# Row sums of the last two expert turns by slot-table products in both layers, and the first filters and spectrum inside the first expert loop

## The chip, the cores and the metric

The kernel runs on one core of a Trainium2 chip, in one launch. The metric is the device time of that launch in microseconds (us), as the median of several runs. All data is f32. The engines are TensorE (PE), VectorE (DVE), ScalarE (ACT), GpSimd (POOL) and SyncE (SP), each with its own instruction queue; they wait for each other by semaphores. DMAs are issued by SP, POOL and ACT.

## What is computed

One step of a trunk with two layers over 384 tokens (128 of a prompt, 256 of a sample) of width 1024. Layer 0 mixes tokens with a gated linear attention and an mLSTM, layer 1 with a Hyena long convolution, computed as a product of spectra. Behind each mixer stands a mixture of 16 experts, of which every token uses two.

```python
def _hyena_mixer(u, p, j):
    z = u @ p['hy_w_in'][j]
    ...
    v, x1, x2 = jnp.split(z.astype(f32), 3, axis=-1)
    kf = _hyena_filters(L, p, j)
    def long_conv(s, o):
        y = jnp.fft.irfft(jnp.fft.rfft(s, n=2 * L, axis=1) * kf[None, :, o], n=2 * L, axis=1)[:, :L]
        return y + bias[o] * s
    y = x2 * long_conv(x1 * long_conv(v, 0), 1)
    return y.astype(u.dtype) @ p['hy_w_out'][j]

def _hier_moe(u, p, l):
    ...
    hg = jnp.einsum('bld,edf->blef', u, p['moe_w_gate'][l])
    hu = jnp.einsum('bld,edf->blef', u, p['moe_w_up'][l])
    h = jax.nn.silu(hg) * hu * gates.astype(u.dtype)[..., None]
    return jnp.einsum('blef,efd->bld', h, p['moe_w_down'][l])

def _trunk(x, cvec, init_states, p):
    for l in range(DEPTH):
        h = _modulate(x, p['norm1_w'][l], sh1, sc1)
        mix = _rec_mixer(...) if l % 2 == 0 else _hyena_mixer(h, p, j)
        x = x + g1 * mix
        h = _modulate(x, p['norm2_w'][l], sh2, sc2)
        x = x + g2 * _hier_moe(h, p, l)
    return _rmsnorm(x, p['norm_f_w']), finals
```

Left out are a convolution with three taps between `z` and the split, and the choice of the experts (a group by argmax, the two best in it, and their weights as `gates`). The Hyena filters do not depend on the tokens: `h` is a small network of the positions, its last matrix is `hy_f_w3`, and the spectrum `kf` follows by products with tables of cosines and sines.

## The kernel before

An expert loop has 16 turns, one for each expert. The 13 experts behind the first three are taken in the order of how many tokens they have, so that a turn has a fixed number of slots for token rows: 96 (three tiles of 32), 64 or 32. Turn 13 has two tiles, turns 14 and 15 have one each; `PICKED` are turns 14 and 15. Token rows are written to `x_rows` in DRAM by slot, read back turn by turn, transposed by PE (`rows_t`), multiplied with gate and up weights (`gate_up`, in two halves of 32 records), then SiLU on ACT, product on DVE, a transpose (`hidden_t`) and `down`. The result of a turn lies in `ysb[:, p % 2]`, copied there by ACT (`rows_out`), with 32 slots in each quarter of the partitions: quarter q holds columns 256 q to 256 q + 255. SP stores it to `y_rows` in DRAM (`store`).

Weights go through a ring of six slots of 2 MB, three for even and three for odd turns, one piece of `down` weights in `uT`. SP issues all of their loads and the stores in one hand-written order: behind the products of turn p come the loads for turn p + 2, then `store(p)`. SP's DMAs run in one queue in this order.

At the end of the loop a token's two rows have to be added with their weights w1 and w2:

- In layer 0 (`token_rows`, `first_rows`, `combined`, `rows_back`, `add_rows`) turns 14 and 15 are stored like the others. POOL then gathers two rows for each token from `y_rows` with six indirect DMAs, ACT scales the first, DVE adds the second, PE transposes the sum, and DVE adds it to the residual stream `xT`. PE fills the time until the rows come with the first filters: `first_taps` and `filters` multiply the small network with `hy_f_w3` (ring slot 0, loaded behind the last expert), DVE scales by a decay into `hpm`, and `spectrum` makes ten products with the tables.
- In layer 1 turns 14 and 15 are not stored. `in_last` and `pick_table` on DVE find out during turns 1 to 3 which tokens have a row in these turns and make a table of slots, which PE transposes in turns 4 to 6 (`pick`). At the end the product of this table with `ysb` (`last_expert`) opens the sum of a token tile in four banks, each with a quarter of the columns, and products of the gathered rows with diagonals of w1 and w2 (`others`) close it. DVE multiplies by the gate, adds to `x_tok` and norms (`final_rows`).

After layer 0 follow the norm and the z products of Hyena (`wide(("z", m), ...)`, 24 times 8 matmuls), with `filters(1)` in front of them on PE. The PSUM banks are given out by `claim`, in an order written out by hand; an engine that wants to write a bank waits until its reader before is through. If more tokens fall on an expert than it has slots (`over > CAP`), a branch of its own computes the rest; it is not taken with the inputs at hand.

## Time and profile before

| | us |
|---|---|
| median of 3 runs | 1237.32 |
| lowest and highest | 1233.12 and 1238.73 |
| span of the profiled execution | 1246.0 |
| PE busy in it | 1118.7 |
| DVE, ACT, POOL busy | 370.7, 213.4, 140.7 |

The profile records one execution: for every instruction its engine, line, start and duration, and for idle time in front of it the engine or DMA whose semaphore ended it. A matmul in f32 leaves two records, a transpose one. The two expert loops run from about 356 to 627 and from 947 to 1218 us. PEclk is the clock granted to TensorE, as a share of its full 2.4 GHz.

### The profile page before, as it was taken

What the parts mean: (1) busy time and instruction counts of PE and PEld (TensorE: products, weight loads), DVE (VectorE), ACT (ScalarE), POOL (GpSimd) and SP (SyncE); (2) the same over time, 40 slices, a digit from 0 to 9 for tenths busy, and PEclk for the clock granted to TensorE, in tenths of its full rate; (3) what the DMA queues carried; (4) which work ended last, traced back from release to release, by engine and by line L of the source; (5) the groups of instructions that cost most, each with busy time, mean ns of one, the idle gap of its engine ahead of it and who ended that gap; (6) DMA issues with size and microseconds to landing.
All of it is one profiled execution on the core that took longest, in us unless ns stands there. A gap on an engine that the chain in (4) does not pass through costs nothing.

```text
span 1246.0 us, 23402 instructions
## 1 busy us (share of the span) xinstructions
PE 1118.7 (90%) x10195; PEld 626.8 (50%) x10195; DVE 370.7 (30%) x954; ACT 213.4 (17%) x449; POOL 140.7 (11%) x163
## 2 busy tenths in 40 slices
PE   5999999899989959898699999999998995989965
PEld 2443445555665525454336665545665553555534
DVE  3202332574341101101047222487624120110104
ACT  2003201320321101111024111121021110111102
POOL 1143100022120000000010000042232000000001
PEclk9899999899989979998879999999998997999988
DMA  9988755369559998999964211001485999899984
GB/s 382 391 294 297 298 201 207 138 210 408 204 199 364 387 379 340 386 399 402 399 224 166 75 61 68 1 0 68 163 356 214 367 383 394 329 389 399 405 360 152
DMA packets 73236, 338.22 MB, mean 271 GB/s; under 512 B 6834, under 2 KB 16593, under 8 KB 58348
## 3 DMA queue, kind: packets, MB, share of 16 engines
q1 hardware_dynamic: 61784, 299.93, 62.3%
q0 software_dynamic: 10864, 36.42, 8.4%
q8 instruction: 82, 1.34, 0.4%
q10 hardware_dynamic: 484, 0.35, 0.1%
q14 instruction: 22, 0.18, 0.0%
HBM read 313.97 MB, written 22.70 MB: 270 GB/s over the span
## 4 chain that ended last, share of the span: by engine, by line
PE 71%; DMA 16%; DVE 6%; ACT 2%; issue 2%; SPq 1%; another core or an unknown queue 1%; DVEq 0%; ACTq 0%
PE ps L2284 19%; PE ps L1995 18%; DMA ring<-in_moe_w_up 12%; PE ps L1917 11%; PE ps L2308 7%; PE ps L2510 3%; DMA ring<-in_ada_w 3%; PE ps L2217 2%; PE ps L1938 2%; DMA ring<-in_hy_f_w 2%; PE ps L2480 1%; PE ps L2321 1%; PE ps L2267 1%; PE ps L1910 1%; PE ps L2294 1%
## 5 line engine op out<-in xcount | busy, mean ns | idle before, releaser
L2284 PE MATMUL ps<-ring,work 128*32 128x256 f32 x4736 | 299.8, 393 | 73.4 <-DMA ring<-in_moe_w_up 65.5
L2284 PEld LDWEIGHTS ps<-ring,work 128*32 128x32 f32 x4736 | 149.6, 112 | 174.4 <-issue 88.8
L1995 PE MATMUL ps<-uT,ring 128*128 128x384 f32 x640 | 217.2, 496 | 2.4 <-DVE uT L1341 1.3
L1995 PEld LDWEIGHTS ps<-uT,ring 128*128 128x128 f32 x640 | 121.7, 194 | 88.0 <-issue 10.8
L2308 PE MATMUL ps<-ring,work 128*32 128x256 f32 x1728 | 102.9, 379 | 1.2 <-issue 1.2
L1763 DVE COPY work<-ps 128x128 f32<-128x128 f32 x74 | 21.5, 290 | 261.4 <-PE ps L2294 261.4
L1917 PE MATMUL ps<-ring,uT 128*128 128x512 f32 x192 | 84.3, 596 | 0.0
L1165 ACT ACTIVATE work<-ps 128x128 f32<-128x128 f32 x74 | 20.5, 278 | 359.3 <-PE ps L2284 346.8
L2308 PEld LDWEIGHTS ps<-ring,work 128*32 128x32 f32 x1728 | 56.1, 110 | 37.9 <-issue 1.5
L1759 DVE TENSOR_TENSOR work<-ps,work 128x128 f32<-128x128 f32 x74 | 21.6, 291 | 161.6 <-ACT work L1165 161.6
L901 POOL DMA_DIRECT2D work<-x_rows x30 | 15.4, 515 | 422.4 <-PE ps L2267 414.5
L1848 DVE SCALAR_TENSOR_TENSOR work<-ps,vecT,work 128x127 f32<-128x127 f32 x96 | 35.5, 412 | 92.4 <-ACT work L1248 91.6
L1917 PEld LDWEIGHTS ps<-ring,uT 128*128 128x128 f32 x192 | 36.1, 191 | 47.6 <-issue 47.6
L1938 PE MATMUL ps<-ring,silc 128*32 128x512 f32 x384 | 48.8, 640 | 5.5 <-DMA ring<-in_ada_w 4.3
L1171 ACT COPY work<-ps 128x256 f32<-128x256 f32 x74 | 27.5, 372 | 114.6 <-PE ps L2308 107.7
L2510 PE MATMUL ps<-uT,ring 128*128 128x384 f32 x128 | 43.3, 491 | 1.2 <-DVE uT L1895 1.2
L1910 PE MATMUL ps<-tab_common,work 128*128 128x128 f32 (+2 forms) x161 | 27.4, 306 | 16.1 <-DMA work<-in_t_pos 10.9
L1917 PE MATMUL ps<-work,ring 128*128 128x128 f32 (+3 forms) x256 | 39.7, 293 | 1.5 <-DVE ring L1882 0.8
L939 POOL TENSOR_TENSOR ring<-ring 128x1024 f32<-128x1024 f32 x4 | 13.6, 3403 | 216.4 <-DVE ring L1871 216.4
L1917 PEld LDWEIGHTS ps<-work,ring 128*128 128x128 f32 (+1 forms) x256 | 32.6, 190 | 8.9 <-PE ps L1917 2.5
L1910 PEld LDWEIGHTS ps<-tab_common,work 128*128 128x128 f32 (+2 forms) x161 | 22.5, 170 | 28.1 <-issue 17.1
L1917 PE MATMUL ps<-work 128*128 128x512 f32 x80 | 36.5, 608 | 0.0
(352 smaller groups left out, 1082.4 us busy)
## 6 DMA issues: line engine op xcount, KB each, us to landing
ring<-in_moe_w_gate SPq DMA_DIRECT2D x32, 2048.0 KB, 12.6
ring<-in_moe_w_up SPq DMA_DIRECT2D x32, 2048.0 KB, 17.6
ring<-in_ada_w SPq DMA_DIRECT2D x24, 2048.0 KB, 11.4
ring<-in_moe_w_down SPq DMA_DIRECT2D x22, 2048.0 KB, 23.3
uT<-in_moe_w_down SPq DMA_DIRECT2D x10, 1536.0 KB, 16.4
ring<-in_rec_w_in SPq DMA_DIRECT2D x6, 2048.0 KB, 23.8
ring<-in_hy_w_in SPq DMA_DIRECT2D x6, 2048.0 KB, 10.8
y_rows<-work SPq DMA_DIRECT2D x64, 96.0 KB, 10.9
```

The lines of the kernel that those rows point to most:

```text
L1171: free(act.copy(ysb[:, p % 2, i, :], bank((l, p, "Y", i))[:, 0:256]), (l, p, "Y", i))
L1759: free(v.tensor_tensor(hh[:, par, :], bank((l, p, "GU", i))[:, P:2 * P], sg[:, par, :], ALU.mult), (l, p, "GU", i))
L1763: free(v.tensor_copy(hT[:, (FIRST[p] + i) % 2, :], bank((l, p, "HT", i))[:, 0:P]), (l, p, "HT", i))
L1848: ins = v.scalar_tensor_tensor(dst[:, a0 + do:a0 + do + n], src[:, a0 + so:a0 + so + n], w, dst[:, a0 + do:a0 + do + n], ALU.mult, ALU.add)
L1910: ins = pe.transpose(bank(key)[0:n, at:at + p], src, ident[0:p, 0:p])
L1917: ins = pe.matmul(out, lhsT, rhs, start=(i == 0), stop=(i == n - 1))
L1938: ins = pe.matmul(bank(key)[32 * q:32 * q + 32, :], silc[:, 2 * two + k, :], w[:, k, q * 512:(q + 1) * 512], start=(two == 0 and k == 0), ...
L1995: ins = pe.matmul(bank(key)[0:rows, 0:T], w(k), uT[:, k, :], start=(k == 0), stop=(k == DC - 1))
L2217: done(pe.matmul(bank(key)[:], h2T[:, j * P:(j + 1) * P], w3[0:65, at:at + 512], start=True, stop=True), key)
L2284: ins = pe.matmul(bank(key)[32 * q:32 * q + 32, 0:2 * P].rearrange("p (a n) -> p a n", a=2), xg[:, u, k, 32 * i:32 * i + 32], ring[:, 3 * ...
L2308: ins = pe.matmul(bank(key)[32 * q:32 * q + 32, 0:256], hT[:, (FIRST[p] + i) % 2, 32 * k:32 * k + 32], w[:, q * 256:(q + 1) * 256], start= ...
L2510: ins = pe.matmul(bank(("ho", m))[:, 0:T], w[:, k, (m % 4) * P:(m % 4 + 1) * P], uT[:, k, :], start=(k == 0), stop=(k == DC - 1))
```

## The change

1. **Layer 0 now does as layer 1.** `in_last`, `pick_table` and the transposes of the table run in both layers. Turns 14 and 15 are stored in neither.
2. **Open row sums.** A bank ("sum", l, j, hf) holds 512 columns of a token tile j. In layer 0 `rows_back` opens it with plain matmuls by the identity (before: transposes), in layer 1 `others` does. `picked(0, j)` adds turn 14 and `picked(1, j)` turn 15. Between matmuls that use different quarters of the array's rows and write the same bank PE waits for its own last matmul (`settle`). `down` of turn 15 stands between the sums of tile 1 and tile 2.
3. **Store and gathers.** The store of turn 13 is issued by ACT (`store_last`) instead of SP. POOL's six gathers wait for it and no longer for turn 15; the loads into ring slots 0, 1 and 2 behind the loop get waits for the readers of what lies there meanwhile.
4. **First filters inside the loop.** The part of `hy_f_w3` for stage 0 is loaded by ACT in turn 6 into `w3s0`; `first_taps(0)` and `filter_weights(0)` run in turn 10. `filters(0)` stands in front of turn 14's `hidden_t` and `down`, and `spectrum(0)` between them and the products of turn 15. `first_taps(1..3)` stand in front of z, `filter_weights(1..3)` behind z 0 to 2, and `filters(1)` behind z 4.
5. **Overflow indices** go to a table of their own (`late`), so `in_last` has 17 chained steps instead of 9. The additions stand in front of the branch and what the branch computes is added once more. ACT's `preload_act_table` stands in front of the branch as well.

The core of the diff:

```diff
+        FILTERS_AT = 4
@@ SP, behind the loop
-                    store(p)
+                    if p < NE - 3:
+                        store(p)
...
-                if l == 0:
-                    for p in PICKED:
-                        store(p)
@@ POOL
-                    for u in range(2):
-                        pool.wait_ge(S(f"y{u}_stored"), 4 * 16 * (NE // 2 * (l + 1) - l))
+                pool.wait_ge(S("picks_known"), l + 1)
+                for u in range(2):
+                    pool.wait_ge(S(f"y{u}_stored"), 4 * 16 * STORED * (l + 1))
+                if l == 0:
+                    full(pool, (0, PICKED[0], "GU", 0))
...
+                        pool.indirect_dma_start(tok_rows[l][q][:, j, :], None, y_dram[0:BASES[PICKED[0]], :],
@@ ACT, behind turn 14's step of the loop
+                store_last()
+                rows_out(PICKED[0], 0)
+                if l == 0:
+                    full(act, (0, NE - 3, "Y", TILES[NE - 3] - 1))
+                    spectrum(0, K_ORDER[0])
+                    first_rows(0)
+                    first_rows(1)
+                silu(PICKED[1], 0)
+                if l == 0:
+                    first_rows(2)
+                act.preload_act_table(ACT.Sqrt)
...
+                rows_out(PICKED[1], 0)
+                if l == 1:
+                    final_squares(0)
@@ DVE, behind turn 14's step of the loop
+                if l == 0:
+                    filters(0)
...
+                hidden_t(PICKED[0], 0)
+                if l == 0:
+                    combined(0)
+                    combined(1)
+                hidden(PICKED[1], 0)
+                hidden_t(PICKED[1], 0)
...
+                if l == 0:
+                    combined(2)
+                    for j in range(NT):
+                        add_rows(j)
+                else:
+                    final_rows()
@@ PE
+                def rows_back(j):
+                    pe.wait_ge(S("y_sum"), j + 1)
+                    for hf in range(2):
+                        key = ("sum", 0, j, hf)
+                        opened(pe, key)
+                        for n in range(4):
+                            m = 4 * hf + n
+                            pe.matmul(bank(key)[:, n * P:(n + 1) * P], utok[:, j, m * P:(m + 1) * P], ident, start=(n == 0), stop=False)
+                def others(j):
+                    pe.wait_ge(S(f"token_rows_{j}"), 32 * (l + 1))
+                    for hf in range(2):
+                        key = ("sum", 1, j, hf)
+                        opened(pe, key)
+                        for c in range(2):
+                            pe.matmul(bank(key)[:], mix_w[:, 2 * j + c, :], tok_rows[1][c][:, j, hf * 512:(hf + 1) * 512],
+                                      start=(c == 0), stop=False)
+                def picked(i, j):
+                    p, last = PICKED[i], i == len(PICKED) - 1
+                    for half in range(2):
+                        for n in range(2) if l == 0 else range(1):
+                            for hf in range(2):
+                                q = 2 * hf + half
+                                rows, key = slice(32 * q, 32 * q + 32), ("sum", l, j, hf)
+                                end = last and half == 1 and n == (1, 0)[l]
+                                if l == 0:
+                                    at = (2 * half + n) * P
+                                    ins = pe.matmul(bank(key)[:, at:at + P], ysb[rows, p % 2, 0, n * P:(n + 1) * P], pick[rows, j, i, :],
+                                                    start=False, stop=end)
+                                else:
+                                    ins = pe.matmul(bank(key)[:, half * 256:(half + 1) * 256], pick[rows, j, i, :], ysb[rows, p % 2, 0, :],
+                                                    start=False, stop=end)
...
+                        if half == 0 or not last:
+                            settle(ins)
+                if l == 0:
+                    pe.wait_ge(S("dft_loaded"), 16)
+                    filters(0)
+                hidden_t(PICKED[0], 0)
+                down(PICKED[0], 0)
+                if l == 0:
+                    spectrum(0, K_ORDER[0])
+                both_halves(PICKED[1], 0)
+                hidden_t(PICKED[1], 0)
...
+                for j in range(2):
+                    (rows_back, others)[l](j)
+                    picked(0, j)
+                down(PICKED[1], 0)
+                (rows_back, others)[l](2)
+                picked(0, 2)
+                evacuated(pe, (l, PICKED[1], "Y", 0))
+                for j in range(NT):
+                    picked(1, j)
```

What stands in a row on PE at the end of layer 0's loop. Before, from turn 15's row transposes (L2267) on; L2284 are halves of gate and up, L2294 `hidden_t`, L2308 `down`, L2205 `first_taps`, L2217 `filters`, L1917 `spectrum` and L1910 `rows_back`:

```order
L2267 MATMUL ps<-tab_common,work 128x32 x8
L2284 MATMUL ps<-ring,work 32x256 x16
L2294 MATMUL ps<-tab_common,work 128x128
L2284 MATMUL ps<-ring,work 32x256 x16
L2308 MATMUL ps<-uT,work 32x256 x12
L2308 MATMUL ps<-work 32x256 x4
L2294 MATMUL ps<-tab_common,work 128x128
L2308 MATMUL ps<-ring,work 32x256 x16
L2205 MATMUL ps<-ring,work 1x512
```

After, from the same place on; L2358 are the row transposes, L2308 `filters(0)`, L2385 `hidden_t`, L2399 `down`, L2003 `spectrum(0)`, L2375 gate and up, L2459 `rows_back`, L2482 `picked`:

```order
L2358 MATMUL ps<-tab_common,work 128x32 x8
L2308 MATMUL ps<-work 128x512 x6
L2385 MATMUL ps<-tab_common,work 128x128
L2399 MATMUL ps<-uT,work 32x256 x12
L2399 MATMUL ps<-work 32x256 x4
L2003 MATMUL ps<-ring,work 128x512 x10
L2375 MATMUL ps<-ring,work 32x256 x32
L2385 MATMUL ps<-tab_common,work 128x128
L2459 MATMUL ps<-tab_common,work 128x128 x8
L2482 MATMUL ps<-work 128x128 x8
L2459 MATMUL ps<-tab_common,work 128x128 x8
L2482 MATMUL ps<-work 128x128 x8
```

`filters(0)`, turn 14's `down` and `spectrum(0)` moved ahead of the products of turn 15.

On ScalarE, between the end of layer 0's loop and the first norm of layer 1. Before (L1222 is the preload, L1233 the squares, L1227 the roots):

```order
L1127 COPY ring<-ps 128x512
L1222 ACT_TABLE_LOAD
L1233 ACTIVATE work<-xT 128x4x128 x4
L1227 ACTIVATE rstd<-ps,eps 128x128
L1233 ACTIVATE work<-xT 128x4x128 x2
```

After, behind the branch (L1289 the squares, L1283 the roots):

```order
L1289 ACT_TABLE_LOAD
L1289 ACTIVATE work<-xT 128x4x128 x4
L1283 ACT_TABLE_LOAD
L1283 ACTIVATE rstd<-ps,eps 128x128
L1289 ACTIVATE work<-xT 128x4x128 x2
```

The preload (now L1247) stands in front of the branch, and two table loads stand behind it.

On PE at the end of layer 1, behind gate and up of turn 15. Before (L2308 is `down` of turn 14 and then of 15, L2433 `last_expert`, L2440 the first of `others`):

```order
L2308 MATMUL ps<-uT,work 32x256 x12
L2308 MATMUL ps<-work 32x256 x4
L2294 MATMUL ps<-tab_common,work 128x128
L2308 MATMUL ps<-ring,work 32x256 x16
...
L2433 MATMUL ps<-work 128x256 x16
L2440 MATMUL ps<-work 128x256
L2440 MATMUL ps<-ring,work 128x256
```

After (L2468 `others`, L2485 `picked`):

```order
L2375 MATMUL ps<-ring,work 32x256 x32
L2385 MATMUL ps<-tab_common,work 128x128
L2468 MATMUL ps<-work 128x512
L2468 MATMUL ps<-ring,work 128x512
L2468 MATMUL ps<-work 128x512
L2468 MATMUL ps<-ring,work 128x512
L2485 MATMUL ps<-work 128x256 x4
```

`others` and turn 14's share now stand ahead of turn 15's `down`.

## Rows read from the trace of the kernel before

**Rows 1.** The page: span, and GB/s in 40 slices of 31.15 us

```profile
span 1246.0 us, 23402 instructions
...
GB/s 382 391 294 297 298 201 207 138 210 408 204 199 364 387 379 340 386 399 402 399 224 166 75 61 68 1 0 68 163 356 214 367 383 394 329 389 399 405 360 152
```

**Rows 2.** Timeline, PE, layer 0: start us, busy us, instruction, [idle before, releaser]

```profile
616.65 3.58 PE L2284 MATMUL ps<-ring,work 128*32 128x256 f32 x32 [10.12 <-DMA ring<-in_moe_w_up]
...
631.42 10.61 PE L2217 MATMUL ps<-ring,work 65*128 65x512 f32 x12
...
645.63 5.42 PE L1917 MATMUL ps<-work 128*128 128x512 f32 x12
...
665.47 5.32 PE L2217 MATMUL ps<-ring,work 65*128 65x512 f32 x12
...
670.63 10.48 PE L1995 MATMUL ps<-uT,ring 128*128 128x384 f32 x32
```

**Rows 3.** Stretches, layer 0: us, busy PE PEld DVE ACT POOL, PEclk, DMA, GB/s

```profile
616.60:620.20 3.60, 3.55 (x33) 1.66 (x33) 0.00 (x0) 0.00 (x0) 0.00 (x0) 0.52 1.12 429
...
631.40:636.00 4.60, 4.60 (x7) 1.99 (x7) 1.38 (x2) 0.00 (x0) 3.38 (x5) 0.50 0.69 198
```

**Rows 4.** Timeline, VectorE (DVE) and ScalarE (ACT), layer 0

```profile
626.75 0.37 ACT L1171 COPY work<-ps 128x256 f32<-128x256 f32 x1 [2.24 <-PE ps L2308]
...
633.61 0.69 DVE L1592 TENSOR_TENSOR work<-ps,work 128x512 f32<-128x512 f32 x1 [2.73 <-PE ps L2217]
...
649.39 1.28 DVE L1814 SCALAR_TENSOR_TENSOR work<-work 128x1024 f32<-128x1024 f32 x1 [0.19 <-ACT work L1132]
...
654.28 1.28 ACT L1222 ACT_TABLE_LOAD   x1
...
657.41 4.22 DVE L1824 SCALAR_TENSOR_TENSOR xT<-ps,ada,xT 128x128 f32<-128x128 f32 x16
...
662.57 0.95 DVE L1316 RECIPROCAL rstd<-rstd 128x128 f32<-128x128 f32 x1 [0.85 <-ACT rstd L1227]
...
667.63 3.26 DVE L1321 SCALAR_TENSOR_TENSOR work<-xT,mA,rstd 128x256 f32<-128x256 f32 x8
```

**Rows 5.** Timeline, PE, the end of layer 1

```profile
1207.09 3.61 PE L2284 MATMUL ps<-ring,work 128*32 128x256 f32 x32 [9.39 <-DMA ring<-in_moe_w_up]
...
1210.88 1.93 PE L2284 MATMUL ps<-ring,work 128*32 128x256 f32 x32
...
1223.00 3.79 PE L2433 MATMUL ps<-work 32*128 32x256 f32 x32 [5.48 <-ACT work L1171]
```

**Rows 6.** Timeline, the other engines, the end of layer 1

```profile
1213.83 0.99 POOL L911 DMA_INDIRECT work<-y_rows,work  x1 [42.66 <-issue]
...
1222.38 0.37 ACT L1171 COPY work<-ps 128x256 f32<-128x256 f32 x1 [6.85 <-remote]
...
1228.41 0.42 DVE L1618 TENSOR_TENSOR work<-ps,work 128x256 f32<-128x256 f32 x1 [12.92 <-PE ps L2440]
...
1241.70 1.29 DVE L1608 SCALAR_TENSOR_TENSOR work<-work 128x1024 f32<-128x1024 f32 x1
```

**Rows 7.** Timeline, attention products with a self-wait: matmuls, and their weight loads (PEld)

```profile
207.18 5.61 PE L2065 MATMUL ps<-ring 64*128 64x128 f32 x48
...
208.77 0.53 PEld L2065 LDWEIGHTS ps<-ring 64*128 64x128 f32 x8 [0.29 <-PE ps L2065]
```

**Rows 8.** Timeline, PE: the first gate and up products of both layers

```profile
356.34 3.61 PE L2284 MATMUL ps<-ring,work 128*32 128x256 f32 x58 [0.61 <-issue]
...
947.29 4.17 PE L2284 MATMUL ps<-ring,work 128*32 128x256 f32 x60 [0.61 <-issue]
```

**Rows 9.** DMA issues, 520 to 610 us: count, KB each, median us to landing

```profile
y_rows<-work SPq DMA_DIRECT2D x12, 64.0 KB, 14.0
...
ring<-in_hy_f_w SPq DMA_DIRECT2D x1, 1024.0 KB, 19.4
...
work<-x_rows POOLq DMA_DIRECT2D x2, 128.0 KB, 5.6
```

409 lines of the change are left out of this document (218 added, 191 removed).

## The prediction, made before the change was run

> **What bounds the kernel now.** I read the page first: over the 1246.0 us DMA moves about 400 GB/s in both expert loops and much less elsewhere [rows 1]. Such a mean does not say what an edit is worth, so the next view was the timeline at the two places which the edit touches, with the granted clock beside it. I call the last three turns of an expert loop 13, 14 and 15.
>
> Layer 0. PE stands 10.12 us for the last `up` weights before it starts turn 15 at 616.65, so it was through with turn 14's gate and up products and turn 15's row transposes at 606.5 [rows 2]. After `down` it waits again, for `hy_f_w3`, which was queued behind those weights and took 19.4 us to land [rows 9]. The wait costs twice: the granted clock is 0.52 in the first product behind it and 0.50 from 631.4 on [rows 3], half speed (1.2 instead of 2.4 GHz). The same twelve records of `filters` take 10.61 us there and 5.32 us at 665.47 at full clock [rows 2]. The residual additions end at 657.41 + 4.22 = 661.6 [rows 4], and the first z product starts at 670.63 [rows 2]. So this stretch is bound by PE in program order behind two late transfers. What is saved before z is saved in the total: no row behind 670 waits for DMA until the next expert loop.
>
> Layer 1. PE waits 9.39 us for the last weights and starts turn 15 at 1207.09 [rows 5]. ScalarE's last copy starts at 1222.38, after 6.85 us put down to a "remote" releaser [rows 6]; the same copy in layer 0 waited 2.24, for PE [rows 4]. The difference, 4.6 us, I can't explain. PE follows at 1223.00 with 32 records in 3.79 us [rows 5]. VectorE works almost without a gap from 1228.41 to 1242.99 and the output goes out [rows 6].
>
> **Layer 0, step by step** (on the clock of the profile). PE now has work at 606.5: `filters(0)`, whose weights lie ready since turn 10, 5.3 at full clock. VectorE scales its last bank (0.69) and copies turn 14's hidden rows (some 0.3); with the flag read that is about 1.4. `down` of 14 has 32 records, as has a half of gate and up, which takes 1.93 [rows 5]: 2.0. Ten spectrum products, 20 records at 5.42/12 = 0.45, are 9.1, to 624.3 [rows 2, 4]. Gate and up of turn 15 are 2 x 1.93 = 3.9. Their weights are there: they landed at 616.65 before, and 7.7 us of delay would still be hidden. SiLU, product and transpose behind two 1.28 combinations: 1.2, to 629.4.
>
> Then the row sums. `rows_back(j)` is 8 matmuls, 16 records of 0.115 (5.61/48 in [rows 7] is 0.117 with waits): 1.85. `picked` has a self-wait (`settle`) between groups of array rows. For that the gate-attention products of layer 0 are the nearest: 8 records take 0.53 of weight loading and then a gap of 0.29 to 0.30 [rows 7]. I take 0.83 per half: 1.65 for each `picked(0, j)` and 1.35 for each `picked(1, j)`. The bounds of a settle are 0 (nothing but the drain that a reader waits for anyway) and 0.30; I take 0.30, because the row is of the same construction. So 2 x 3.5 + `down` 1.9 + 3.5 + 1.35 brings the first complete sum to 643.2. VectorE adds three tiles, 24 x 0.27 = 6.5 (4.22/16 each, [rows 4]), to 649.7.
>
> From the end of the additions to the first z product: before, reciprocals and scaling ran 661.6 to 667.63, and the first chunk would have been there at about 668.4 if `filters(1)` had not held PE to 670.8. That is 6.8, of which 0.85 was a wait; 6.1 without it [rows 4]. ScalarE now loads a table in between, since the branch is behind the preload, 1.28 each [rows 4]. The first of the two loads is hidden in the wait for the sums, the second delays the root by some 0.4. z starts at 656.2 instead of 670.6: 14.4 saved. `filters(1)` moves into the z loop behind z 4, where PE has no gap: 5.3 back. `filter_weights(1..3)`, 3 x 2.1 on VectorE, go beside z products of 5.8 us in which VectorE has 1.7 of work: nothing. Layer 0: **-9.1**.
>
> In the loops: the small load of `hy_f_w3` (0.26 MB at 0.41 MB/us) falls into a saturated queue, +0.6. `in_last` grows from 9 to 17 chained VectorE steps of 0.2 each, in both layers. The loop of layer 1 has the shorter one and the picks already, and needs 1207.09 - 947.29 = 259.8 from first to last product against 616.65 - 356.34 = 260.3 in layer 0 [rows 2, 5, 8]: that work has cover. The longer chain (3.5 us behind a copy, before the next one is due) exceeds it by some 0.3 four times, half of it on the path: +0.6. The four stores of turn 13 go from SP's queue to ScalarE's. I count some 2 us for their issue, at a time when nothing waits for ScalarE (its next work is 8 us away).
>
> **Layer 1, step by step.** The store of turn 13 no longer stands behind 6 MB of weights. DMAs on GpSimd's queue of 128 KB land in 5.6 us in the saturated loop, while SP's stores need about 14 [rows 9]. So turn 13 is stored near 1204, the six gathers start near 1205 instead of 1213.83, and their bytes flow from about 1207.3 (2.5 us after the issue, as before). The store's bytes push the last weights by 0.4: turn 15 at 1207.5. Gate and up 5.5, cold again as in [rows 5], hidden part 1.2: 1214.2. Now `others(j)`, 8 records of 0.45 = 3.6, and `picked(0, j)` 1.65, three times: 15.75; `down` 1.9; `picked(1, 0)` 1.35: first sum at 1233.2. VectorE then needs 3 x 2.86 (two pairs of 128x512, at the 0.69 of [rows 4]), two scalings of 1.45, ScalarE's squares and root 1.5 and the last scaling 1.45, less overlap: 13.05, against 14.6 in 256-wide pieces. End 1246.3 instead of 1243.0: **+3.3**. What before stood in the shade of the late ScalarE copy is now PE work in a row, and nine settles are new. The preload and ScalarE's own last copy are off this path.
>
> Sum: -9.1 + 0.6 + 0.6 + 3.3 = -4.6 us of the profiled 1246.0, so 1241.4 there. That execution is 8.7 longer than the median of the three runs, 1237.32; taking the same difference, **1232.7**.
>
> **Rivals.** (a) The 4.6 us of the "remote" stall belong to the profiled execution alone. For it: no row names a cause, the same copy in layer 0 had none [rows 4], and the profiled span is 8.7 over the median. Then layer 1 loses 7.9 and all comes to 1237.3: no change. (b) The row sums are cheaper: settles overlap with the neighbouring group (9 x 0.3 in each layer), and the last transfers in layer 1 finish as before: 4 to 5 us less, 1228. (c) Slower: the gathers go ahead of the last weights in layer 1. 3.15 MB at 0.41 MB/us are 7.7 us; if they were served first, turn 15 would start at 1214.8 and everything behind it 7.3 later: 1240.0, over the time before. It decides when more than 4.6 us of the gathers' bytes overtake `up`. Against it: the bytes begin only when `up` has landed (1206.84 before); for it: the store could land at 1200 already, with GpSimd's queue free. Its milder form: with the bytes on the way from 1203 and half of the rate for each queue, `up` is late by 3 to 4 us, 1236 in all. Together with (a) the full form is 1244.6.
>
> The Trainium skill bears on (c). "DMA: Bandwidth & Descriptors", in "Queues, rings and completion order", says that each DMA engine takes turns between the queues that have work, packet by packet. The landing times of [rows 9] agree: a small load on another queue does not wait for the megabytes on SP's. By that rule an early gather gets half of the rate and not all of it, which is the milder form of (c); no row shows gathers and weights on the way together.
>
> (d) That the change doesn't do what it says: PE finds no work at 606.5 because a filter bank is not free or the store on ScalarE's queue is late. The claims show banks 0, 2, 4, 6, 7, 1, all read by 606.9; a late gather is needed only at 625, some 5 us after I expect it.
>
> **Chances.** Forecast 0.50, own range 1229.5 to 1236; (a) 0.17; (b) 0.18; (c) in both forms, also with (a), 0.12; (d) 0.03. The range is 1226 to 1241. A measurement of this kernel can tell about 0.5%, 6.2 us, from no change. Faster than 1231.1 are (b) and a good third of the forecast: 0.38. Slower than 1243.5 is (c) with (a), and (d): 0.09. Within 0.5%: 0.53.
>
> **What would show it.** Right: in layer 0 PE works from 606 to 645 without a gap over 2 us at a granted clock of 1.00; z starts 14 us sooner after turn 14; z's loop has one break of 5.3. In layer 1 turn 15 starts within 1 us of 1207 (counted from the loop's first product), and the first addition on VectorE comes 25 to 26 us behind it. Wrong: a second wait for `up` in layer 0, a clock of 0.5 in the spectrum or in the first z product (up to 3 us), settles far from 0.30, or gathers that push turn 15 of layer 1. If VectorE's last scaling ends at most 36 us behind the start of turn 15 as before, the term of +3.3 was wrong.

## The result and the profile after

The changed kernel takes 1253.5 us (median of 4: 1244.9 to 1259.0), the kernel before 1236.2 timed beside it (median of 4): a ratio of 1.0139, 95% interval 1.0095 to 1.0182. Forecast were 1232.7 and a range of 1226 to 1241, so both the size and the sign are wrong. The first profile of after is its fastest execution (1244.9, span 1243.0) and hides the loss: it starts the first expert loop 4 us sooner than the profile of before, a difference that lies ahead of anything the change touches. Two more profiles of after, from other chips, have spans of 1260.7 and 1261.4; they are among the slowest executions of their kernel. I therefore count every stretch from a mark of its own: the first gate and up product of a loop, turn 15's first one, the first z product, and the end of VectorE's last scaling.

Where the time is, in us (before: five profiles, one of them of before_row; after: three; the kernels are those of the experiments; every row is one execution):

| profile | layer 0: loop to turn 15 | turn 15 to z | z to layer 1's loop | layer 1: loop to turn 15 | turn 15 to end | all |
|---|---|---|---|---|---|---|
| before | 260.3 | 54.0 | 276.7 | 259.8 | 35.9 | 886.7 |
| before, four more | 260.2 to 261.1 | 53.5 to 56.2 | 275.4 to 276.8 | 261.7 to 262.8 | 36.1 to 36.5 | 888.3 to 892.8 |
| forecast for after | 268.6 | 31.9 | 282.0 | 260.8 | 38.8 | 882.1 |
| after (first) | 268.1 | 36.1 | 280.6 | 261.4 | 41.1 | 887.4 |
| after_again | 269.1 | 48.3 | 282.2 | 261.0 | 44.9 | 905.5 |
| after_third | 268.0 | 46.8 | 280.6 | 263.4 | 44.7 | 903.4 |
| store_on_sp | 270.9 | 49.4 | 280.6 | 261.8 | 47.2 | 909.8 |
| gathers_x | 271.5 | 35.0 | 280.6 | 264.6 | 38.8 | 890.5 |
| silu_first | 267.4 | 36.0 | 282.2 | 260.9 | 41.8 | 888.3 |
| held | 266.1 | 42.3 | 282.2 | 259.1 | 40.7 | 890.3 |
| l1_rows_last | 268.0 | 46.7 | 280.6 | 261.8 | 45.1 | 902.2 |
| l0_rows_last | 267.8 | 39.8 | 283.4 | 264.0 | 44.8 | 899.8 |
| both_rows_last | 270.6 | 36.8 | 281.9 | 262.5 | 42.1 | 893.9 |
| l1_by_block | 271.2 | 39.7 | 282.2 | 262.9 | 41.9 | 897.9 |
| old_l1 | 266.8 | 48.3 | 282.2 | 259.4 | 27.6 | 884.4 |
| mix | 268.8 | 37.7 | 280.6 | 261.4 | 27.7 | 876.2 |
| mix_free | 269.3 | 39.2 | 282.1 | 260.4 | 33.9 | 885.0 |
| before_early | 260.3 | 53.2 | 276.6 | 262.2 | 33.5 | 885.7 |

In these profiles two cells of after carry the loss: turn 15 to z, and turn 15 to the end. First TensorE at the end of layer 0, in the fast profile; it answers to [rows 2]:

```profile
602.98 5.42 PE L2308 MATMUL ps<-work 65*128 65x512 f32 x12
...
611.61 8.85 PE L2003 MATMUL ps<-ring,work 128*128 128x512 f32 x20
620.39 3.66 PE L2375 MATMUL ps<-ring,work 128*32 128x256 f32 x64
626.81 0.30 PE L2385 MATMUL ps<-tab_common,work 128*128 128x128 f32 x1 [2.76 <-DVE work L1822]
...
656.53 10.56 PE L2081 MATMUL ps<-uT,ring 128*128 128x384 f32 x32 [0.62 <-ACT uT L1296]
```

The part that was meant to work does: `filters(0)` (L2308) and the spectrum (L2003) stand where the wait for `up` was, at full clock, and turn 15 (L2375) starts without a wait. The same place in after_third:

```profile
622.61 3.51 PE L2375 MATMUL ps<-ring,work 128*32 128x256 f32 x47
626.48 1.25 PE L2375 MATMUL ps<-ring,work 128*32 128x256 f32 x17 [0.36 <-issue]
637.27 0.45 PE L2385 MATMUL ps<-tab_common,work 128*128 128x128 f32 x1 [9.54 <-DVE work L1822]
637.61 3.75 PE L2459 MATMUL ps<-tab_common,work 128*128 128x128 f32 x16
```

TensorE stands 9.54 us in front of turn 15's transpose (L2385), with VectorE's product (L1822) as releaser. ScalarE shows what that product waits for (L1157 scales gathered rows, L1190 is turn 15's sigmoid, L1205 turn 13's store), and GpSimd when the gathers begin:

```profile
605.18 1.79 ACTq L1205 DMA_DIRECT2D y_rows<-work  x4
...
625.15 1.15 ACT L1157 ACTIVATE work<-work 128x1024 f32<-128x1024 f32 x1 [1.85 <-DMA ring<-y_rows,work]
634.38 1.15 ACT L1157 ACTIVATE work<-work 128x1024 f32<-128x1024 f32 x1 [8.09 <-DMA ring<-y_rows,work]
635.44 0.26 ACT L1190 ACTIVATE work<-ps 128x128 f32<-128x128 f32 x1
```

```profile
617.98 1.00 POOL L923 DMA_INDIRECT work<-y_rows,work  x1 [37.19 <-DMA y_rows<-work]
```

The sigmoid's input was ready at 627.73, but in ScalarE's order it stands behind `first_rows(1)`, which waits 8.09 us for the second pair of gathers. The gathers began 12.8 us behind the issue of the store they wait for. The stall is paid twice: the granted clock behind it is 0.57 (the column behind the busy times), and 16 records of `rows_back` take 3.75 us, where they take 2.05 at full clock.

```profile
637.00:643.00 6.00, 5.66 (x33) 5.09 (x33) 1.70 (x3) 2.43 (x2) 0.00 (x0) 0.57 1.05 386
```

In layer 1 the first row of TensorE that touches gathered rows (L2468) waits for them in the fast profile; the last additions of VectorE (L1672) begin behind the last slot-table products (L2485). These answer to [rows 5, 6]:

```profile
1208.24 1.10 PE L2468 MATMUL ps<-work 128*128 128x512 f32 x2 [2.73 <-DMA ring<-y_rows,work]
...
1224.05 4.72 PE L2485 MATMUL ps<-work 32*128 32x256 f32 x32
...
1227.18 0.69 DVE L1672 TENSOR_TENSOR work<-ps,work 128x512 f32<-128x512 f32 x1 [21.34 <-PE ps L2485]
...
1238.37 1.29 DVE L1660 SCALAR_TENSOR_TENSOR work<-work 128x1024 f32<-128x1024 f32 x1
```

### The profile page after: what moved, and what is told of

It is laid out like the page before. It is cut to its first block, busy times and chain, and to the rows that moved or that the text cites. A ratio compares the mean times of both kernels' runs of the same rounds, so it can differ in the third digit from the quotient of the medians.

```text
span 1243.0 us, 23662 instructions
## 1 busy us (share of the span) xinstructions
PE 1118.7 (90%) x10297; PEld 624.7 (50%) x10297; DVE 377.5 (30%) x993; ACT 217.2 (17%) x454; POOL 140.6 (11%) x163
## 4 chain that ended last, share of the span: by engine, by line
PE 70%; DMA 17%; DVE 6%; ACT 2%; issue 2%; SPq 1%; POOL 1%; ACTq 0%; DVEq 0%; POOLq 0%
PE ps L2375 17%; PE ps L2081 17%; PE ps L2003 11%; DMA ring<-in_moe_w_up 10%; PE ps L2399 7%; PE ps L2627 3%; DMA ring<-in_ada_w 3%; PE ps L2024 2%; DMA y_rows<-work 2%; PE ps L2597 1%; PE ps L2308 1%; PE ps L2358 1%; PE ps L2385 1%; PE ps L1996 1%; DMA ring<-y_rows,work 1%
## 5 line engine op out<-in xcount | busy, mean ns | idle before, releaser
L2375 PE MATMUL ps<-ring,work 128*32 128x256 f32 x4736 | 298.0, 396 | 57.5 <-DMA ring<-in_moe_w_up 52.9
L2375 PEld LDWEIGHTS ps<-ring,work 128*32 128x32 f32 x4736 | 150.5, 113 | 158.7 <-issue 72.6
L2081 PE MATMUL ps<-uT,ring 128*128 128x384 f32 x640 | 214.2, 491 | 3.0 <-DVE uT L1391 1.3
L2081 PEld LDWEIGHTS ps<-uT,ring 128*128 128x128 f32 x640 | 120.2, 191 | 87.8 <-issue 10.1
L2399 PE MATMUL ps<-ring,work 128*32 128x256 f32 x1728 | 102.9, 379 | 0.1
L2003 PE MATMUL ps<-ring,uT 128*128 128x512 f32 x192 | 84.1, 595 | 0.0
L1190 ACT ACTIVATE work<-ps 128x128 f32<-128x128 f32 x74 | 20.5, 277 | 337.8 <-PE ps L2375 337.8
L2399 PEld LDWEIGHTS ps<-ring,work 128*32 128x32 f32 x1728 | 55.4, 110 | 38.0 <-DVE work L1826 0.8
L1822 DVE TENSOR_TENSOR work<-ps,work 128x128 f32<-128x128 f32 x74 | 21.6, 292 | 160.8 <-ACT work L1190 160.8
L2003 PEld LDWEIGHTS ps<-ring,uT 128*128 128x128 f32 x192 | 35.9, 190 | 46.8 <-issue 46.8
L2627 PE MATMUL ps<-uT,ring 128*128 128x384 f32 x128 | 43.3, 491 | 1.2 <-DVE uT L1981 1.2
L2003 PE MATMUL ps<-work,ring 128*128 128x128 f32 (+3 forms) x256 | 39.7, 293 | 1.5 <-DVE ring L1968 0.8
L2003 PEld LDWEIGHTS ps<-work,ring 128*128 128x128 f32 (+1 forms) x256 | 32.5, 190 | 8.9 <-PE ps L2003 2.5
L1996 PE MATMUL ps<-tab_common,work 128*128 128x128 f32 (+2 forms) x143 | 23.7, 294 | 13.7 <-DMA work<-in_t_pos 10.9
L1304 ACT ACTIVATE work<-ps,vecT 128x384 f32<-128x384 f32 x24 | 13.9, 580 | 112.9 <-PE ps L2081 112.9
L2627 PEld LDWEIGHTS ps<-uT,ring 128*128 128x128 f32 x128 | 23.7, 190 | 17.8 <-issue 3.0
## 6 DMA issues: line engine op xcount, KB each, us to landing
ring<-in_moe_w_up SPq DMA_DIRECT2D x32, 2048.0 KB, 17.7
ring<-in_ada_w SPq DMA_DIRECT2D x24, 2048.0 KB, 11.4
y_rows<-work SPq DMA_DIRECT2D x64, 96.0 KB, 12.7
```

What stands on the lines that cost most here:

```text
L1190: act.activation(sg[:, (FIRST[p] + i) % 2, :], bank((l, p, "GU", i))[:, 0:P], ACT.Silu).then_inc(S("silu_out"), 1)
L1822: free(v.tensor_tensor(hh[:, par, :], bank((l, p, "GU", i))[:, P:2 * P], sg[:, par, :], ALU.mult), (l, p, "GU", i))
L1996: ins = pe.transpose(bank(key)[0:n, at:at + p], src, ident[0:p, 0:p])
L2003: ins = pe.matmul(out, lhsT, rhs, start=(i == 0), stop=(i == n - 1))
L2081: ins = pe.matmul(bank(key)[0:rows, 0:T], w(k), uT[:, k, :], start=(k == 0), stop=(k == DC - 1))
L2375: ins = pe.matmul(bank(key)[32 * q:32 * q + 32, 0:2 * P].rearrange("p (a n) -> p a n", a=2), xg[:, u, k, 32 * i:32 * i + 32], ring[:, 3 * ...
```

## The experiments

Kernels timed together shared a chip and its runs of before. The ratios below are to those, with the 95% interval. The groups are: before_again, after_again, store_on_sp, before_row (before 1248.6 us); gathers_x and the three with `rows_last` (1247.4); silu_first, held, old_l1, mix (1236.9); after_third, before_early, mix_free, l1_by_block (1246.4).

**Controls.** before_again is before, after_again and after_third are after, before_row is before with one edit:

```diff
-        x_dram = nc.dram_tensor("x_rows", [XROWS, D], F32).ap()
+        x_dram = nc.dram_tensor("x_rows", [XROWS + 1, D], F32).ap()
...
```

> The kernel before, unchanged, timed against itself on the chip that the other kernels of this call use. It gives the spread of one kernel here and a second profile of before, to be laid beside the first, whose span (1246.0) was above all four plain times (1233.1 to 1238.7). Theory A (the changed kernel is really slower, and the first profile of before was a slow copy): the plain times stay within some 6 us of each other around 1236, and the new profile has a span near 1234. Theory B (a pair of executions differs by 10 us and more whatever the kernel, so the 1.4% are chance): the times of this kernel spread over 12 us or more.

> The changed kernel, unchanged, again. Theory A: 1.4% slower than before again (1.009 to 1.018), its own times spread over 10 us and more, and a profile with a longer span than the first one of after (1243.0) shows in which stretch the added time lies. Theory B: within 0.5% of before. By the prediction's sum it would be 0.4% faster.

> The kernel before with the table of rows for the experts made one row (4 KB) longer in DRAM, as the change has it, and nothing else; no instruction differs, only where the tables behind it lie. Theory P (part of the loss is where the rows lie in DRAM, since every gather, store and scatter goes there): slower than before by more than 0.5%. Otherwise: the same as before within 0.3%.

> The changed kernel, unchanged, on the chip of the other kernels of this call, as the measure for them: 0.8% to 1.4% slower than before if the two earlier comparisons hold, its profile with a stretch from turn 15's first product to the end of 41 to 45 us in layer 1.

before_again 0.9978 (0.9946 to 1.0010), before_row 0.9992 (0.9963 to 1.0021): where the rows lie in DRAM costs nothing that these runs can tell. after_again 1.0079 (1.0044 to 1.0114), after_third 1.0093 (1.0057 to 1.0129): after is slower on all three chips, by 0.8 to 1.4%. Theory A's guess that before spreads over 6 us only was wrong: its 28 times on this chip go from 1234.5 to 1253.2, the spread that theory B named. But theory B's conclusion, that the difference is chance, does not hold: on three chips the interval of after lies above 1.

**The queue of turn 13's store** (store_on_sp):

```diff
-                    if p < NE - 3:
-                        store(p)
+                    store(p)
...
-                store_last()
```

> The changed kernel with one part undone: the store of turn 13's rows goes out on SyncE's queue in the step of turn 13, as in the kernel before, and not on ScalarE's at the start of turn 15. Theory C (the extra 10 us are this store: it lands 9 to 10 us after its issue beside the weight loads, so the gathers of the token rows start late, share the engines with the first loads for the Hyena layer, and the sums of the rows wait for them in some executions): the store is issued earlier than in after by some 2 us but behind the last weight loads, the gathers move, and the time falls by 5 us or more against after, and its spread with it. Theory D (the store's queue does not matter, the time is lost in the expert loops or in the waits between row groups): the same as after within 3 us.

1.0208 (1.0163 to 1.0254), 14.5 us slower than after_again beside it. Theory C had the wrong sign. In layer 1 the gathers begin 7.0 us behind turn 15's first product instead of 2.4, and the end is 47.2 us behind it. In layer 0 they begin 3.2 us ahead of turn 15 instead of 4.7. So the store on ScalarE's queue is a gain of the change, and the time of the gathers matters on both ends. The two profiles differ by only 4.3 us from the first loop to the end, so they don't show all of the 14.5.

**What the gathers' wait costs** (gathers_x; the edit in layer 0, in layer 1 a wait for turn 13's `down` takes the place of the one for its store; left out is that the sums get the right rows):

```diff
-                for u in range(2):
-                    pool.wait_ge(S(f"y{u}_stored"), 4 * 16 * STORED * (l + 1))
+                pool.wait_ge(S("y0_stored"), 4 * 16 * STORED * (l + 1))
...
-                        pool.indirect_dma_start(tok_rows[l][q][:, j, :], None, y_dram[0:BASES[PICKED[0]], :],
+                        pool.indirect_dma_start(tok_rows[l][q][:, j, :], None, x_dram[0:BASES[PICKED[0]], :],
```

> The changed kernel, but in both layers the gathers of the token rows read the table of the experts' input rows instead of their output rows, so that they need not wait for turn 13's store and start some 12 us earlier in layer 0 (14 in layer 1); all else the same. Left out of the computation: the sums get rows of the wrong table. Theory G (the loss is the chain store of turn 13, 10 to 16 us until it has landed, then the gathers, 6 to 10 us each, which ends on TensorE's path: in layer 0 through the scaling of gathered rows that stands ahead of turn 15's sigmoid on ScalarE, in layer 1 at the first product with gathered rows): faster than the changed kernel by 15 us or more (its layer 0 tail falls from 36 to 48 us behind turn 15's first product to under 35, TensorE waits in layer 1 for no gather), so 3 to 8 us under before. Theory R (the loss is the many waits between row groups, the longer sum on VectorE, or the loops): within 4 us of the changed kernel.

1.0007 (0.9983 to 1.0032). Against 0.8 and 0.9% for after on the two chips with like times of before this is 9 to 11 us: theory G with about two thirds of the price it named. Turn 15 to z is 35.0, to the end 38.8, and TensorE waits for no gather. What stays are 890.5 us from the first loop to the end, as much as before has: with the gathers free of charge the change would gain nothing. Its loops to turn 15 are 1.2 to 3.6 us longer than in the three profiles of after.

**Order of the sums** (l1_rows_last, l0_rows_last, both_rows_last): slot-table products first, those with gathered rows last. Where layer 0 is changed, ScalarE's sigmoid of turn 15 and the copy of its rows, and VectorE's product, also stand ahead of the gathered rows. The order on TensorE, shown for a kernel that has it in both layers:

```diff
-                for j in range(2):
-                    (rows_back, others)[l](j)
-                    picked(0, j)
-                down(PICKED[1], 0)
-                (rows_back, others)[l](2)
-                picked(0, 2)
-                evacuated(pe, (l, PICKED[1], "Y", 0))
-                for j in range(NT):
-                    picked(1, j)
+                down(PICKED[1], 0)
+                for j in range(NT):
+                    picked(0, j)
+                evacuated(pe, (l, PICKED[1], "Y", 0))
+                for j in range(NT):
+                    picked(1, j)
+                for j in range(NT):
+                    (rows_back, others)[l](j)
```

> The changed kernel with another order in layer 1 alone: turn 15's down product straight behind its transpose, then the slot-table products of both last turns, which open the sums, and the products with the gathered rows last, which close them. No work is added or left out but two waits between row groups. Theory G: TensorE no longer waits for the gathers beside idle work, and the first sum closes 4 us behind the landing of the first gathers instead of some 19 us: 8 to 12 us faster than the changed kernel, since the 13 us of VectorE's closing work start that much earlier. Theory R: the same number of waits and of products, the first sum no earlier than TensorE is through with all products: within 3 us of the changed kernel.

> The changed kernel with another order in layer 0 alone: turn 15's sigmoid and its product ahead of the scaling and adding of gathered rows on ScalarE and VectorE, and on TensorE turn 15's down product and all slot-table products ahead of the products that turn the gathered rows back. Theory G: nothing of turn 15 stands behind a gather any more; against the changed kernel the stretch from turn 15's first product to z falls from 36 to 48 us to 34 to 40, so 4 to 10 us faster, and the plain times lie closer together. Theory R: no gain, since the same products and waits between row groups follow in a row: within 3 us.

> Both orders together. Theory G: the gains add up to 12 to 22 us against the changed kernel, which would make it faster than before by 5 us or more. Theory R: within 4 us of the changed kernel, so slower than before.

1.0078 (1.0048 to 1.0108), 1.0052 (1.0034 to 1.0070), 1.0070 (1.0046 to 1.0095). Theory G expected 8 to 12 us from layer 1 and found none: the end stays 45.1 us behind turn 15. The timeline and the stretch of l1_rows_last show why:

```profile
1227.71 13.33 PE L2498 MATMUL ps<-work 32*128 32x256 f32 x48
```

```profile
1227.70:1241.10 13.40, 12.59 (x52) 5.22 (x48) 0.00 (x0) 0.37 (x1) 0.00 (x0) 0.61 0.00 1
```

48 records take 13.33 us; in the fast profile of after the same 48 take 7.66, as 8, 8 and 32 (1.47, 1.47 and 4.72). The granted clock is 0.61 in this stretch, between the levels of 1.2 and 2.4 GHz, and 1.00 in after's. Three more settles, at 0.3 each, are under 1 us of the difference. Here the 48 stand in a row behind a wait and have 32 array rows each; in after the products of `others`, with 128, stand between and ahead of them. What the order won, the clock took. In layer 0 the order did shorten the stretch to z (36.8 and 39.8 against 46.7 on this chip), by 7 to 10 us in the profiles; but the medians are only 1 to 2 us under that of l1_rows_last, which the intervals don't tell apart.

**Order by block** (l1_by_block: `down` of turn 15 first, then `others(j)`, `picked(0, j)`, `picked(1, j)` for each j).

> The changed kernel with another order in layer 1 alone: turn 15's down product straight behind its transpose, then for each block of 128 tokens the products with gathered rows, the slot-table products of turn 14 and of turn 15, so that the first block's sum closes before the second block's begins; banks and waits between row groups stay as changed. Theory Y (the cost of the new end is the order: all products of turn 15's rows last, so that the first sum closes behind nearly everything): the first addition comes 17 to 21 us behind turn 15's first product, the end 33 to 37 us, and the time falls by 5 to 9 us against the changed kernel. Theory Z (it is the waits between row groups, which hold TensorE at half clock or stretch the products): the end stays over 40 us behind, within 3 us of the changed kernel.

1.0068 (1.0038 to 1.0097): 3.9 us less than after_third beside it. The first addition comes 21.4 us behind turn 15's first product, near theory Y's 17 to 21, but the next sums close 6.5 and 8.3 us later, and VectorE waits for them: an end of 41.9, not 33 to 37. The order is worth some 3 us.

**The old form of the sums in layer 1** (old_l1):

```diff
+                for q in range(4):
+                    if l == 1:
+                        claim(("sum", 1, j, q), 4 * (j % 2) + q)
...
+                    last_expert(0)
+                    last_expert(1)
+                    others(0)
+                    others(1)
+                    last_expert(2)
+                    others(2)
```

> The changed kernel with the end of layer 1 as in the kernel before: down product of turn 15, then sums of 256 columns in four banks each, opened by the slot-table products of both turns without waits between row groups, closed by the products with gathered rows; layer 0 and the early store stay as changed. Theory U (the new end of layer 1 costs 6 to 10 us where the prediction had 3.3: in the profiles, from turn 15's first product to the end, 41 to 48 us and 36 before): 5 to 9 us faster than the changed kernel, and the end lies 34 to 37 us behind turn 15's first product. Theory V (the end of layer 1 costs what was predicted): 2 to 4 us.

0.9986 (0.9955 to 1.0016), 16.6 us under silu_first, which has the new form and was timed on the same chip. The end is 27.6 us behind turn 15. TensorE's slot-table products (L2471) in old_l1, and VectorE's first addition:

```profile
1222.78 2.01 PE L2471 MATMUL ps<-work 32*128 32x256 f32 x32 [0.48 <-ACT work L1200]
```

```profile
1225.98 0.42 DVE L1676 TENSOR_TENSOR work<-ps,work 128x256 f32<-128x256 f32 x1 [5.87 <-PE ps L2478]
```

Four sums of 256 columns, each with its own 32 array rows in a bank of its own, need no self-wait: 32 records in 2.01 us where the new form takes 4.72. And VectorE can add the first quarter 13.1 us behind turn 15's first product, where it starts at 28.6 in after. That is not the gathers alone: in gathers_x, where TensorE waits for none, it starts at 26.3, since in the new form nearly all products stand ahead of the first closed sum.

This is the largest effect in the medians. Restoring the sums of layer 1 alone takes the whole loss away (old_l1), while no edit of layer 0 does (silu_first and held below, 1.0111 and 1.0101 on the same chip).

**Layer 0: sigmoid first, loads held** (silu_first: ScalarE's `silu` and VectorE's `hidden` of turn 15 ahead of the gathered rows; held: SyncE waits for `token_rows_0` to `_2` ahead of `hy_f_w3`; mix: both and old_l1; mix_free: mix without held).

```diff
                     spectrum(0, K_ORDER[0])
-                    first_rows(0)
-                    first_rows(1)
                 silu(PICKED[1], 0)
                 if l == 0:
-                    first_rows(2)
+                    for j in range(NT):
+                        first_rows(j)
...
```

> The changed kernel with turn 15's sigmoid (ScalarE) and its product (VectorE) in layer 0 ahead of the scaling and adding of the gathered rows; TensorE's order is untouched. Theory Q (turn 15's sigmoid stands behind a gather that has not landed: 7 to 9 us in the slower profiles, 0.9 in the fast one): the transpose of turn 15 comes within 2 us of its last gate product in every profile; but TensorE then waits for the first sum to be turned back, so only a part of the 7 to 9 us comes back, 1 to 4 us against the changed kernel. Theory R (no part of it): within 1 us.

> The changed kernel, but SyncE holds the first loads for the Hyena layer (w3 and four of its input weights) back until the gathers of layer 0 have landed. Theory S (the gathers are slow because these loads share the engines with them): the third gather lands 5 to 8 us earlier (within 12 us of the gathers' start, not 20), the stretch from turn 15's first product to z falls under 40 us, and the time by 4 to 10 us against the changed kernel. Theory T (the gathers take their 6 to 10 us anyway, or the loads come too late for z): no gain, or z waits for its weights.

> The three edits of this call together: sigmoid first, loads held, the old end of layer 1. If theories Q, S and U hold, their gains add up to 10 to 20 us against the changed kernel, so it is 2 to 8 us faster than before; if they do not, it is no faster than before.

> As mix, but without holding the first loads for the Hyena layer back. If holding them back matters beside sigmoid first, it is 1 to 5 us slower than mix was against before (0.3% faster); if not, the same, 0.2% to 0.5% faster than before.

silu_first 1.0111 (1.0075 to 1.0147), held 1.0101 (1.0064 to 1.0138): after was not timed on their chip, so a gain of 1 to 4 us can't be told. The profiles tell the mechanism. With the loads held the three pairs are there 7.4, 10.3 and 12.9 us behind the first gather's issue, against 7.2, 16.4 and 20.3 in after_third, and these are ScalarE's rows of held:

```profile
625.48 1.15 ACT L1159 ACTIVATE work<-work 128x1024 f32<-128x1024 f32 x1 [2.08 <-DMA ring<-y_rows,work]
628.38 1.15 ACT L1159 ACTIVATE work<-work 128x1024 f32<-128x1024 f32 x1 [1.76 <-DMA ring<-y_rows,work]
630.90 1.15 ACT L1159 ACTIVATE work<-work 128x1024 f32<-128x1024 f32 x1 [1.21 <-DMA ring<-y_rows,work]
```

So the loads beside them cost the gathers 7.4 us (5.8 against the fast profile, where the third pair is there after 18.7). "DMA: Bandwidth & Descriptors" of the Trainium skill says in "Queues, rings and completion order" that an engine takes turns between queues packet by packet. The rows agree that both queues move on at the same time, but the gathers lose more than half of their rate: pairs two and three need 5.4 us in held and 13.2 in after_third. What DMA moves in all also falls, to 223 GB/s in the 9.2 us for which the second pair is awaited, against 277 ahead of it and 389 behind:

```profile
625.15:634.30 9.15, 2.12 (x24) 0.64 (x19) 1.28 (x1) 1.15 (x1) 0.13 (x1) 0.87 0.99 223
```

Which pair pays is decided by when the second pair is issued. In after (first), silu_first, mix_free and l1_by_block its second gather is issued 2.4 to 2.6 us ahead of SyncE's load of `hy_f_w3`, and ScalarE can scale the pair 9.8 to 11.4 us behind the first gather's issue. In after_again, after_third, store_on_sp, old_l1 and l1_rows_last it is issued between 1.1 us ahead and 0.5 behind, and the pair comes after 16.1 to 17.7 us. The third pair comes late in both groups (18.7 to 21.8).

Turn 15 to z falls to 42.3 only in held, not under 40. With sigmoid first it is 36.0 to 39.2 in the three kernels that have it here, and holding the loads adds nothing on top: mix 0.9969 (0.9943 to 0.9995), mix_free 0.9975 (0.9957 to 0.9994). These two beat both kernels, by 3 to 4 us against before.

**The early store alone** (before_early: before, with turn 13's store of layer 1 on ScalarE's queue behind its copy):

```diff
-                    store(p)
+                    if l == 0 or p < NE - 3:
+                        store(p)
...
+                    if l == 1 and p == NE - 2:
...
+                            act.dma_start(dst[q], ysb[32 * q:32 * q + 32, 1, 0:n, :]).then_inc(S("y1_stored"), 16)
```

> The kernel before with one part of the change alone: in layer 1 the store of turn 13's rows is issued on ScalarE's queue as soon as they are copied, not on SyncE's queue. Theory W (with the old form of the sums the early store is worth the 8 us by which the end of layer 1 is shorter in old_l1 and mix, 27.6 us, than in before, 35.9): the gathers start 2 to 3 us behind turn 15's first product, not 6.7, the late copy of turn 15's rows on ScalarE that stands in all profiles of before (4.6 us behind its product) may go, and the time falls by 3 to 8 us against before. Theory X (the 8 us come from elsewhere): within 2 us of before.

0.9987 (0.9958 to 1.0016), no difference that can be told: the gathers begin 2.4 us behind turn 15's first product as theory W said, but the end comes at 33.5, not 28. Like for like the early store is worth 2.4 to 3.0 us of the end. ScalarE waits before the sigmoid instead, for a releaser that is not in the profile:

```profile
1214.56 0.28 ACT L1166 ACTIVATE work<-ps 128x128 f32<-128x128 f32 x1 [19.86 <-remote]
```

The product that it reads ends at 1211.01: 3.6 us, the stall of [rows 6] at another place. mix_free has the same form of sums and the same early store as before_early, and differs in the layer 0 part with the sigmoid first (and, in layer 1, in that turn 14's `down` and the preload stand elsewhere). So the pair prices the layer 0 part on one chip: 1243.3 against 1243.8 us. z starts 5.0 us sooner (308.5 behind the loop's start, not 313.5), and the stretch to layer 1's loop is 5.5 longer, `filters(1)`: nothing, where the forecast had 9.1.

**The "remote" stall** (before_p3, before_p4: before again).

> One more profile of the kernel before, unchanged. In the profiles so far the first 128 gate and up products of an expert loop take either 7.0 us or 10.6 to 12.5, and which of the two goes with the chip: on one chip of the first kind before takes 1236.9 us, on three of the second 1246 to 1249. All profiles of before are of the second kind. Theory C1 (on a chip of the first kind the late last copy of layer 1, 4.6 us behind its product, is absent in before too): if this run falls on such a chip, the span is near 1236, and the end of layer 1 lies 29 to 32 us behind turn 15's first product instead of 36. Theory C2: the end is 36 us there as well. If it falls on a chip of the second kind, it only adds a fourth profile like the others, and this stays open.

> The same as before_p3, once more, because that run fell on a chip of the second kind. On a chip of the first kind (7.0 us for the first 128 products of a loop) theory C1 expects a span near 1236 and an end of layer 1 of 29 to 32 us behind turn 15's first product, theory C2 36 us.

Both fell on chips of the second kind: the first 128 records of their loops took 11.5 to 12.7 us, the end was 36.3 and 36.5 behind turn 15. Whether before has the stall on a chip of the first kind stays open. What the other profiles say: on chips where those records took 7.1 us (after, silu_first, held, old_l1, mix) the stall is in none; on the others it is in all but store_on_sp and gathers_x: at ScalarE's last copy in before, at the sigmoid in the changed kernels and in before_early, there 1.7 to 4.6 us long. The two kinds at the first loop's start, after and after_again:

```profile
352.25 7.11 PE L2375 MATMUL ps<-ring,work 128*32 128x256 f32 x128 [0.61 <-issue]
```

```profile
351.80 5.53 PE L2375 MATMUL ps<-ring,work 128*32 128x256 f32 x71 [0.61 <-issue]
357.62 1.12 PE L2375 MATMUL ps<-ring,work 128*32 128x256 f32 x6 [0.29 <-issue]
...
```

In the second TensorE stutters: a few products, then a gap that nothing in the profile explains; its 128 records take 11.5 us. In a loop that is bound by its weights most of this is caught up with (with the change the loops to turn 15 are some 2 us longer on average on chips of the second kind); at the end of layer 1 it is not: old_l1 and mix end 27.6 and 27.7 behind turn 15, mix_free with the same form and a 4.4 us stall 33.9.

## Why the prediction was wrong

Two steps failed: the term of layer 1, +3.3, and in layer 0 the sentence on the late gather. What TensorE does, product by product, was sized right in both layers.

**The step that failed in layer 1: "End 1246.3 instead of 1243.0: +3.3".** The new end was to be 38.8 us behind turn 15, the first addition 25 to 26; gathers_x, without a wait for gathers, has 38.8 and 26.3. But the gathers begin 2.4 us behind turn 15's first product, and I had them 2.5 ahead of it. That, the stall at the sigmoid and the half clock behind it (0.58 in after_third) make 44.7 to 44.9 us, and 41.1 without the stall. And the +3.3 set a new end without a stall against an old end with one, since "the preload and ScalarE's own last copy are off this path". The stall did not go with the copy: it moved to the sigmoid, which is on the path. Like for like the new end is 8.6 us longer (44.8 against 36.2). It consists of two edits that I had priced as one: the early store, 2.4 to 3.0 us of gain (before_early), and the new form of the sums, a loss of 11 us (44.8 against 33.5 and 33.9, with the stall) to 13 or 14 (40.7 to 41.8 against 27.6 and 27.7, without). In the medians it is 16.6 us (silu_first against old_l1), the largest single loss of the change.

**The step that failed in layer 0: "a late gather is needed only at 625, some 5 us after I expect it".** I took the landing of GpSimd's 128 KB loads (5.6 us, [rows 9]) for two other things. The store on ScalarE's queue took 11.1 to 12.8 us until the gathers could begin. And six gathers of 512 KB, beside `hy_f_w3` and the Hyena weights from SyncE, have landed only after 19 to 20 us, of which I had put none on the path: the text names the two combinations ahead of SiLU, with their busy time but not with what they wait for. This is 11 to 12 us in after_again and after_third, 2 to 4 of them through the clock. In the fast profile the gathers began 6.3 us ahead of turn 15's first product, in the other two 4.6 and 4.7, and the scaling waited 1.80 us for the second pair, not 7.70 and 8.09: a start under 2 us earlier, ahead of SyncE's load, made 6 us. Four plain times of one kernel over 14 us fit that, but no run shows that it is their cause.

**Layer 0, what was right.** Turn 15 was to come 268.6 behind the loop's start; it came at 268.1, 269.1 and 268.0. From there to VectorE's first addition 18.9 were expected; gathers_x has 19.0. `rows_back` takes 2.05 for 1.85, `picked(0, j)` 1.50 for 1.65. The additions take 6.29, not 6.5.

**From the additions to z: 3.2 us short.** 6.5 us were expected, 9.7 came (gathers_x: 648.8 to 658.50). TensorE stands 3.1 us between its last slot-table product and the norm in after, 2.95 in gathers_x. The norm's first product needs the first square alone, which in after was there at 642.9, and the table load was over before. What fills the gap is TensorE's own branch on the overflow flag, which the change puts right in front of the norm. It starts at 643.1 and lasts 2.79 us, and the norm starts at 646.02:

```profile
L2515 PEldq COMPARE_BRANCH  x1: 2787/2787/2787, 643.1 to 643.1; - x1
```

The same branch took 0.46 us in before, and takes 0.37 and 0.79 in l0_rows_last and both_rows_last; why it is long here is open. In gathers_x the norm behind it has a granted clock of 0.68 and its 48 records take 8.00 us, against 5.78 at 1.00 in both_rows_last. I had charged 0.4 for a table load, which was not paid (in gathers_x the root waits 2.31 us for TensorE after the load), and nothing for the branch or the clock. It is most of the 4.2 us by which even the fast profile misses.

**Layer 0 as a whole: -9.1 forecast, nothing measured.** In mix_free nothing of turn 15 stands behind a gather, and turn 15 to z is still 39.2 us, not 31.9: 1.84 are a wait for VectorE's first combined rows, 3.0 are row sums below full clock (8.57 us for what takes 5.57 in gathers_x), 2.5 lie between additions and z. With `filters(1)` in the z loop that leaves no gain against before_early (1243.3 and 1243.8 us).

**What the profiles overstate.** The profiled executions of after_again, after_third and old_l1 (1262.5, 1263.2 and 1245.8) lie 4 to 11 us over the medians of their kernels. mix reaches z 10.6 us sooner behind turn 15 than old_l1 in the profiles and is 2.2 us faster in the median; for both_rows_last and l1_rows_last it is 9.9 and 1.3. So the wait of 11 to 12 us ahead of the sigmoid belongs to the slower executions. The medians put most of the loss on the new sums of layer 1; how much of the 9 to 11 us of gathers_x lies in which layer no run shows.

**Hyena: right.** +5.3 for `filters(1)` in the z loop, +3.9 to +5.5 came. **Loops:** +1.2 in both is less than profiles of one kernel differ by.

**The rivals.** (a), the stall belongs to certain executions, is the nearest, though on the level of chips: before takes 1236 to 1237 on two chips and 1246 to 1253 on the others, and all its profiles show the stutter of the latter. That before has no stall on the former would explain why the loss is 1.4% there and 0.8 to 0.9% elsewhere; no profile shows it. Nor is it the chip alone: 5 of the 28 times of before on the first of the slower chips are 1234.5 to 1240.3. The price of (a), no change, was far too low all the same. (b) is refuted: the settles cost about what the row said. (c) did not happen: turn 15 of layer 1 is hardly late (261.0 to 263.4 behind the loop's start against 259.8 to 262.8). It had the gathers in the way of the weights, and it was the weights of the next stage that stood in the way of the gathers. (d) did not happen as told, TensorE had its work at once; but the late store that it names did come, and it was dismissed with the sentence that failed.

Sum for the profile of after_third against the forecast's 882.1: -0.6 loop of layer 0, +14.9 turn 15 to z, -1.4 Hyena, +2.6 loop of layer 1, +5.9 end, together +21.3 but for rounding: 903.4.

## What to carry to other kernels

An engine's program order makes its waits common property: before an operation on the critical path is left behind another, ask not how long that one takes but what it waits for, and follow that chain (store, gather, scaling) with durations of transfers of the same size beside the same traffic. Where an edit is made of two, price each by itself. Before a stretch of a profile is taken as the price of a loss, see where that execution lies among the plain times, and undo the edit alone: here one execution gave 10 us for what was worth 2 in the median. A stall without a cause is not gone because the instruction that showed it is off the path.

## What the runs showed of the hardware

- The same program's first 128 gate and up records of a loop take 7.1 us on some chips and 10.7 to 12.7 on others, in all four profiles of each chip that has four, with gaps put down to "issue"; medians of before differ by 10 us between them. The cause was not found.
- 48 records of products of 32 rows with self-waits: 13.33 us at a granted clock of 0.61, in a row; 7.66 at 1.00 between 128-row products. Without self-waits, in banks of their own, 32 such records take 2.01 us, with them 4.72.
- Six gathers of 512 KB: the last has landed after 12.9 us with SyncE's next loads held back, after 18.7 to 21.8 beside 1 and 2 MB loads on another queue. A pair issued about when the 1 MB load is comes some 6 us later than one issued 2.4 us ahead of it, and DMA as a whole moves 223 GB/s meanwhile. Four stores of 64 KB on ScalarE's queue, issued beside the last weights, are waited for 11.1 to 12.8 us.
- TensorE's branch on the overflow flag: 2.19 to 2.91 us where it stands behind the last slot-table products and in front of the norm (twelve profiles), 0.2 to 0.8 in other places and orders. Nothing in the profile explains the difference.
